# Seven products of block sums for 4 of 16 k tiles of gate/up, and the turn of hid on the tensor engine

## The chip, the cores and the metric

One of the eight cores of a Trainium2 chip runs the whole kernel. The metric is the device time of one launch in microseconds (us), as the median of three runs. The profile is of one execution. Its engines are PE (TensorE, matmuls; PEld is its weight load), DVE (VectorE), ACT (ScalarE), POOL (GpSimd) and SP, which only issues DMAs.

## The reference, cut to what matters

256 tokens of width 2048 pass a sparse attention layer, a layer norm, and a SwiGLU block of hidden width 5632. The change is in the SwiGLU:

```python
x = _layer_norm(DEEPNORM_ALPHA * x + m, ln1_g, ln1_b)             # 256 x 2048, m from the mixer
x = _layer_norm(DEEPNORM_ALPHA * x + (silu(x @ w_gate) * (x @ w_up)) @ w_down, ln2_g, ln2_b)
```

with w_gate and w_up 2048 x 5632 and w_down 5632 x 2048, all float32.

## The kernel before

**Precision.** Every weight is split in two parts of the tensor engine's rounded fp32 type: ACT copies raw to `w_hi` (L627), and DVE takes raw minus `w_hi` as `w_lo` (L903). A product of a 128x128 tile of activations (stationary) and 128x512 of weights (moving) is three matmuls: x_hi by w_hi, x_hi by w_lo, x_lo by w_hi (`product`, L1324 to L1331).

**Gate/up.** The hidden width is cut into 22 tiles of 256 columns (TILES). For a tile, 256 gate and 256 up columns stand side by side: a k tile's weights are 128x512. There are 16 k tiles (KD) and two groups of 128 tokens (TOK), so a tile is 16 x 2 x 3 = 96 matmuls into two PSUM banks of `acc`, with the pair of banks alternating from tile to tile. The weights come in loads of 1 MB (4 k tiles) into a ring `raw` of 4 slots; each load is split in two halves of 2 k tiles, and the split halves stand in rings of 4 (`w_hi`, `w_lo`). A half is thus 12 matmuls, and a tile 8 halves. SP issues a load when both halves of the load four places before it are split (`load`, L392). ACT may write a half's place when PE has used the half four before it (L626).

**After a tile.** While PE works on the next tile, ACT writes `sig` = silu(gate) (L686), DVE `hid` = `sig` times up (L1037), DVE turns `hid` into `turned` by 16 instructions that transpose 32x32 blocks (L1047), ACT writes the hi part of `turned` into `hid_t` (L690) and DVE the lo part (L1053). PE has no part in this. Tile 0 is worked out in an order of its own, between the halves of the layer norm (`first_tile`, L1470 to L1495); tile 1 follows (L1510), and then a loop over pairs of tiles (L1511). PE itself turns the layer norm's result into `act_t` by transposes against `ident` (L1420).

**Down.** Then 4 column groups of 512, each 44 k tiles of `hid_t` by 2 token groups by 3 matmuls (L1527 on). Each engine runs its instructions in the order in which they are written; a wait on a semaphore holds up all that stands behind it on that engine, SP's loads too.

Of the kernel before, what the change touches and what calls it, by code (L numbers as in the profile page):

```python
# [24 lines left out]
F32 = mybir.dt.float32  # L25
# [107 lines left out]
USED_DOWN = USED_FFN + 3 + (TILE_HALVES - 1) * (TILES - 1)  # L133
# [20 lines left out]
def layer_kernel(nc, a):  # L154
    ctx = ExitStack()
    with ctx:
# [7 lines left out]
        raw = sb("raw", [P, RING, RAW_ELEMS])  # L164
# [84 lines left out]

        ssq = small[:, 0:4]  # L250
# [17 lines left out]
        raw_full = [sem(f"raw_full{i}") for i in range(RING)]  # L268
# [68 lines left out]
        ffn_lo = sem("ffn_lo")  # L337
        y_scaled = sem("y_scaled")
# [5 lines left out]
            .rearrange("p (n e) -> p n e", e=IN_COLS)  # L344
        hid_flat = hid_t[:].rearrange("p k h s -> p (k h s)")
# [4 lines left out]
        w_out_rows, w_gu_rows, w_down_rows = flat("w_out"), flat("w_gu"), flat("w_down")  # L350

# [10 lines left out]
        def hid_of(i, x):  # L362
            tile = hid_flat[:, bass.ds(i * 4 * S, 4 * S)].rearrange("p (c x s) -> p c x s", c=2, x=2)
            return tile[:, :, x, :]

# [25 lines left out]
        def _(sp):  # L391
# [32 lines left out]
            with sp.Fori(0, TILES) as i:  # L424
                for j in range(RING):
                    load(R_FFN + RING * i + j, j, RAW_ELEMS,
                         w_gu_rows[bass.ds(i * P, P), j * RAW_ELEMS:(j + 1) * RAW_ELEMS])

            def load_down(g, b):
                k0, k1 = DOWN_K0[2 * b], DOWN_K0[2 * b] + DOWN_K[2 * b] + DOWN_K[2 * b + 1]  # L430
                load(R_DOWN + DOWN_BLOCKS * g + b, b % RING, (k1 - k0) * GC,
                     w_down_rows[bass.ds(g * P, P), k0 * GC:k1 * GC])
# [25 lines left out]
        def _(act):  # L458
# [162 lines left out]
            def hi_loop(used, raw_count, half, slot, n=HALF, first=None):  # L621
# [5 lines left out]
                act.activation(w_hi[:, (2 * slot + half) % RING, 0:n], raw[:, slot, first:first + n],  # L627
                               ACT.Copy).then_inc(hi_done, 1)
# [55 lines left out]
            def silu_step(i, c):  # L684
                act.wait_ge(ffn_full, i + 1)
                act.activation(sig[:], acc[:, 2 * c:2 * c + 2, 0:FC], ACT.Silu).then_inc(ffn_sig, 1)  # L686

            def hid_hi(i):
                act.wait_ge(ffn_turned, i + 1)
                act.activation(hid_of(i, 0), turned[:], ACT.Copy).then_inc(ffn_hi, 1)  # L690

            def ffn_tile(i, c):
                for h in range(TILE_HALVES):
                    used = used_ffn(i - 1, h + RING) if h < RING else used_ffn(i, h - RING)
                    hi_loop(used, fills(R_FFN + h // 2) + i, h % 2, h // 2)
                    if h == 3:
                        silu_step(i - 1, 1 - c)
                    if h == 6:
                        hid_hi(i - 1)

            ffn_tile(1, 1)
            with act.Fori(1, TILES // 2) as i:
                ffn_tile(2 * i, 0)
                ffn_tile(2 * i + 1, 1)


            def down_half(h, g):
                n = len(DOWN_K)
                used = used_down(g, h - 4) if h >= 4 else \
                    used_ffn(TILES - 1, h + 4) if isinstance(g, int) and g == 0 else used_down(g - 1, h + n - 4)  # L710
                hi_loop(used, fills(R_DOWN + h // 2) + DOWN_BLOCKS // RING * g, h % 2, h // 2 % RING,
                        n=DOWN_K[h] * GC, first=h % 2 * HALF)

            for h in range(len(DOWN_K)):
                down_half(h, 0)
                if h == 3:
                    silu_step(TILES - 1, 1)
                if h == 6:
                    hid_hi(TILES - 1)
# [6 lines left out]
            for h in range(HELD + RING, len(DOWN_K)):  # L726
                if h % 2 == 0:
                    act.wait_ge(raw_full[h // 2 % RING],
                                16 * fills(R_DOWN + DOWN_BLOCKS * (COL_GROUPS - 1) + h // 2))
# [14 lines left out]
        def _(dve):  # L744
# [154 lines left out]
            def lo_loop(v, half, slot, n=HALF, first=None):  # L899
                first = half * n if first is None else first  # L900
                dve.wait_ge(hi_done, v + 1)
                h = (2 * slot + half) % RING
# [132 lines left out]
            def gate_up(i, c):  # L1035
                dve.wait_ge(ffn_sig, i + 1)
                dve.tensor_tensor(hid[:], sig[:], acc[:, 2 * c:2 * c + 2, FC:2 * FC], ALU.mult).then_inc(ffn_hid, 1)  # L1037

            def turn_hid(i, to):

                if to[0] == 0:
                    dve.wait_ge(ffn_hid, i + 1)
                for b in to:
                    for n in range(4):
                        src = hid[32 * n:32 * n + 32, :, :].rearrange("p t (c f) -> p t c f", c=2)
                        dst = turned[32 * b:32 * b + 32, :, :].rearrange("p c (t s) -> p t c s", t=TOK)
                        last = dve.transpose(dst[:, :, :, 32 * n:32 * n + 32], src[:, :, :, 32 * b:32 * b + 32])  # L1047
                if to[-1] == 3:
                    last.then_inc(ffn_turned, 1)

            def hid_lo(i):
                dve.wait_ge(ffn_hi, i + 1)
                dve.tensor_tensor(hid_of(i, 1), turned[:], hid_of(i, 0), ALU.subtract).then_inc(ffn_lo, 1)  # L1053

            def ffn_tile(i, c):
                for h in range(TILE_HALVES):
                    lo_loop(2 * R_FFN + TILE_HALVES * i + h, h % 2, h // 2)
                    if h == 3:
                        gate_up(i - 1, 1 - c)
                        turn_hid(i - 1, (0, 1))  # L1060
                    if h == 4:
                        turn_hid(i - 1, (2, 3))
                    if h == 6:
                        hid_lo(i - 1)

            ffn_tile(1, 1)
            with dve.Fori(1, TILES // 2) as i:
                ffn_tile(2 * i, 0)
                ffn_tile(2 * i + 1, 1)


            for g in range(COL_GROUPS):
                for h in range(len(DOWN_K)):
                    v, n = 2 * R_DOWN + len(DOWN_K) * g + h, DOWN_K[h] * GC
# [3 lines left out]
                    else:  # L1078
                        lo_loop(v, h % 2, h // 2 % RING, n=n, first=h % 2 * HALF)
                    if g == 0 and h == 3:  # L1080
                        gate_up(TILES - 1, 1)
                        turn_hid(TILES - 1, (0, 1))
                    if g == 0 and h == 4:
                        turn_hid(TILES - 1, (2, 3))
                    if g == 0 and h == 6:
# [40 lines left out]
        def _(pool):  # L1126
# [39 lines left out]
            pool.wait_ge(xt_full, TOK * CHUNKS)  # L1166
# [5 lines left out]
        def _(pe):  # L1172
# [324 lines left out]
            def ffn_tile(i, c):  # L1497

                if not (isinstance(i, int) and i == 1):
                    pe.wait_ge(ffn_hid, i - 1)  # L1500
                for h in range(TILE_HALVES):
                    pe.wait_ge(lo_done, 2 * R_FFN + TILE_HALVES * i + h + 1)
                    for n in range(2):
                        for t in range(TOK):
                            last = product(2 * c, t, act_t, 2 * h + n, (w_hi, w_lo), h % RING, n,
                                           (h, n) == (0, 0), (h, n) == (TILE_HALVES - 1, 1))
                    last.then_inc(*((pe_used, 1) if h < TILE_HALVES - 1 else (ffn_full, 1)))

            first_tile()
            ffn_tile(1, 1)  # L1510
            with pe.Fori(1, TILES // 2) as i:  # L1511
                ffn_tile(2 * i, 0)
                ffn_tile(2 * i + 1, 1)


            def down_half(g, h, tokens):

                parts = (down_hi, down_lo) if g == COL_GROUPS - 1 and h >= HELD + RING else (w_hi, w_lo)
                for n in range(DOWN_K[h]):
                    k = DOWN_K0[h] + n  # L1520
                    for t in tokens:
                        paused = g == COL_GROUPS - 1 and t == 1 and h == HELD - 1 and n == DOWN_K[h] - 1
                        last = product(2 * (g % 2), t, hid_t, k, parts, h % RING, n, k == 0,
# [3 lines left out]
            def down_group(g):  # L1527
# [3 lines left out]
                pe.wait_ge(ffn_hid, TILES - 1 + g % 2)  # L1531
                held = HELD if g == COL_GROUPS - 1 else len(DOWN_K) - 1
                for h in range(held):
                    pe.wait_ge(lo_done, 2 * R_DOWN + len(DOWN_K) * g + h + 1)
                    if g == 0 and h == 0:
                        pe.wait_ge(ffn_lo, TILES - 1)
                    down_half(g, h, both).then_inc(pe_used, 1)
                for t in both:
                    if g == COL_GROUPS - 1 and t == 1:
                        pe.wait_ge(res_done, 2 * TOK * COL_GROUPS - 1)  # L1540
                    for h in range(held, len(DOWN_K)):
                        if t == 0:
                            pe.wait_ge(lo_done, 2 * R_DOWN + len(DOWN_K) * g + h + 1)
# [58 lines left out]
```

## Time and profile before

| what | us |
|---|---|
| median of 3 runs (lowest, highest) | 953.99 (953.26, 954.17) |
| span of the profiled execution, first to last instruction | 952.0 |
| PE busy in the profiled execution | 946.2 |
| DVE busy | 633.8 |
| ACT busy | 441.9 |
| tiles 1 to 21 and down, one unbroken stretch of PE | 696.33 |

The profiled execution has only its span; no time of the whole launch is recorded for it. The median of the runs is 2.0 us above the span. A matmul's duration in the profile is its latency: the next one starts before it ends, so what a matmul costs PE in a stream is read from start to start.

### The profile page before, as it was taken

To read this page: it belongs to the slowest core of one execution; us is meant where nothing else is said; L and a number is where in the kernel's file an instruction comes from. 1 tells how busy PE (TensorE), PEld (TensorE's weight loads), DVE (VectorE), ACT (ScalarE), POOL (GpSimd) and SP (SyncE) were. 2 spreads that over 40 slices of the span, in tenths; PEclk is the share of its full clock that TensorE was granted. 3 is DMA by queue.
4 is the path that set the end of the run, shared out by engine and by line. 5 is a ranking of instruction groups with operands and counts; after the bars stand their busy time and mean duration, and the time that the engine had idled before them with its cause. 6 is when DMAs were issued, how large, how long until landed. Compare 5 with 4: busy or idle time off the path is not lost.

```text
span 952.0 us, 12299 instructions
## 1 busy us (share of the span) xinstructions
PE 946.2 (99%) x4508; PEld 793.8 (83%) x4508; DVE 633.8 (67%) x1012; ACT 441.9 (46%) x573; POOL 40.9 (4%) x43
## 2 busy tenths in 40 slices
PE   9999999999999999999999999999999999999997
PEld 8999988888888888888888888888888888888885
DVE  6778566588776677777776776677775454554556
ACT  5676764362544444444444444444444343343450
POOL 0105530000000000000000000000000000000000
PEclk9999999999999999999999999999999999999999
DMA  9735225583365555554455555545457465464632
GB/s 365 318 140 177 97 82 185 209 347 142 108 219 204 180 203 190 186 209 178 176 184 211 204 193 185 210 178 194 181 209 291 141 232 188 160 237 156 225 129 88
DMA packets 28128, 183.57 MB, mean 193 GB/s; under 512 B 3136, under 2 KB 3648, under 8 KB 8640
## 3 DMA queue, kind: packets, MB, share of 16 engines
q1 hardware_dynamic: 28064, 183.12, 52.7%
q8 instruction: 22, 0.36, 0.2%
q14 instruction: 10, 0.08, 0.0%
q0 software_dynamic: 32, 0.00, 0.0%
HBM read 181.01 MB, written 2.10 MB: 192 GB/s over the span
## 4 chain that ended last, share of the span: by engine, by line
PE 99%; DVE 0%; ACT 0%; DVEq 0%; issue 0%; ACTq 0%
PE acc L1327 82%; PE acc L1265 5%; PE acc L1186 4%; PE acc L1464 2%; PE acc L1299 1%; PE tp L1378 1%; PE tp L1313 1%; PE tp L1391 1%; PE tp L1175 0%; PE tp L1404 0%; PE tp L1403 0%; PE tp L1402 0%; PE tp L1420 0%; PE acc L1555 0%; PE tp L1233 0%; DVE stats L1107 0%
## 5 line engine op out<-in xcount | busy, mean ns | idle before, releaser
L903 DVE TENSOR_TENSOR w_lo<-raw,w_hi 128x1024 fp32r<-128x1024 f32 (+1 forms) x283 | 335.3, 1194 | 242.4 <-ACT w_hi L627 240.6
L627 ACT ACTIVATE w_hi<-raw 128x1024 fp32r<-128x1024 f32 (+1 forms) x276 | 285.7, 1036 | 403.2 <-PE acc L1327 401.1
L1327 PE MATMUL acc<-w_hi,act_t 128*128 128x512 f32 x1344 | 413.9, 389 | 0.0
L1327 PEld LDWEIGHTS acc<-w_hi,act_t 128*128 128x128 f32 x1344 | 252.3, 188 | 52.5
L1327 PE MATMUL acc<-w_lo,act_t 128*128 128x512 f32 x672 | 261.4, 389 | 0.0
L1327 PE MATMUL acc<-w_hi,hid_t 128*128 128x512 f32 x672 | 207.2, 389 | 0.0
L1327 PEld LDWEIGHTS acc<-w_lo,act_t 128*128 128x128 f32 x672 | 126.1, 188 | 26.1
L1327 PEld LDWEIGHTS acc<-w_hi,hid_t 128*128 128x128 f32 x672 | 126.1, 188 | 26.1
L1327 PE MATMUL acc<-w_lo,hid_t 128*128 128x512 f32 x336 | 130.7, 389 | 0.0
L1047 DVE STREAM_TRANSPOSE turned<-hid 32x128 f32<-32x128 f32 x352 | 106.6, 303 | 5.6
L1327 PEld LDWEIGHTS acc<-w_lo,hid_t 128*128 128x128 f32 x336 | 63.1, 188 | 13.2
L1327 PE MATMUL acc<-w_hi,o_t 128*128 128x512 f32 x224 | 73.4, 398 | 0.0
L1327 PEld LDWEIGHTS acc<-w_hi,o_t 128*128 128x128 f32 x224 | 42.1, 188 | 8.6
L1327 PE MATMUL acc<-w_lo,o_t 128*128 128x512 f32 x112 | 43.6, 390 | 0.0
L779 DVE TENSOR_TENSOR w_lo<-raw,w_hi 128x1024 fp32r<-128x1024 f32 x24 | 29.1, 1219 | 7.7 <-ACT w_hi L489 7.7
L1265 PE MATMUL acc<-cq_t,w_hi 128*128 128x256 f32 x160 | 31.1, 289 | 0.0
L489 ACT ACTIVATE w_hi<-raw 128x1024 fp32r<-128x1024 f32 x24 | 25.0, 1051 | 3.9 <-DMA raw<-in_w_qidx 3.9
L1162 POOL TENSOR_SCALAR prob<-prob,row_inv 128x128 f32<-128x128 f32 (+1 forms) x24 | 25.2, 1063 | 26.7 <-DVE row_inv L877 26.7
L1265 PEld LDWEIGHTS acc<-cq_t,w_hi 128*128 128x128 f32 x160 | 25.2, 188 | 1.1 <-issue 1.0
L1327 PEld LDWEIGHTS acc<-w_lo,o_t 128*128 128x128 f32 x112 | 21.1, 188 | 4.1
L866 DVE TENSOR_TENSOR o_t<-tp,o_t 128x256 fp32r<-128x256 f32 x16 | 6.8, 425 | 25.1 <-ACT o_t L604 25.1
L1265 PE MATMUL acc<-cq_t,w_lo 128*128 128x256 f32 x80 | 22.5, 281 | 0.0
(179 smaller groups left out, 740.1 us busy)
## 6 DMA issues: line engine op xcount, KB each, us to landing
raw<-in_w_gu SPq DMA_DIRECT2D x88, 1024.0 KB, 4.8
raw<-in_w_down SPq DMA_DIRECT2D x32, 1024.0 KB, 4.6
raw<-in_w_out SPq DMA_DIRECT2D x16, 1024.0 KB, 4.8
raw<-in_w_down SPq DMA_DIRECT2D x16, 768.0 KB, 4.0
raw<-in_x_w SPq DMA_DIRECT2D x14, 552.0 KB, 7.1
raw<-in_w_uq SPq DMA_DIRECT2D x4, 1024.0 KB, 6.0
raw<-in_w_ukv SPq DMA_DIRECT2D x4, 1024.0 KB, 5.7
ln_rows<-in_ln_rows SPq DMA_DIRECT2D x4, 1024.0 KB, 7.3
```

Source lines behind the costliest of these rows:

```text
L489: act.activation(split_place(v)[0][:, v % RING, :], raw[:, r % RING, half * HALF:(half + 1) * HALF], ACT.Copy).then_inc(hi_done, 1)
L627: act.activation(w_hi[:, (2 * slot + half) % RING, 0:n], raw[:, slot, first:first + n], ACT.Copy).then_inc(hi_done, 1)
L779: dve.tensor_tensor(w_lo[:, v % RING, :], raw[:, r % RING, half * HALF:(half + 1) * HALF], w_hi[:, v % RING, :], ALU.subtract).then_inc(lo ...
L903: dve.tensor_tensor(w_lo[:, h, 0:n], raw[:, slot, first:first + n], w_hi[:, h, 0:n], ALU.subtract).then_inc(lo_done, 1)
L1047: last = dve.transpose(dst[:, :, :, 32 * n:32 * n + 32], src[:, :, :, 32 * b:32 * b + 32])
L1162: pool.tensor_scalar(prob[:, s % 3, cols], prob[:, s % 3, cols], row_inv[:, (s + 1) % 2, t:t + 1], None, ALU.mult).then_inc(prob_done, 1)
L1186: last = pe.matmul(acc[:, 2 * t + b, 0:c1 - c0], x[:, tok], w[:, c0:c1], start=(k == 0 and x is hi_ and w is hi_), stop=(k == KD - 1 and x ...
L1265: last = pe.matmul(out, part[:, v % RING, e0:e0 + P], act_tiles[:, k, x, :], start=(half == 0 and k == 0 and x == 0 and part is hi_), stop ...
L1299: last = pe.matmul(acc[:, (m + t) % 4, :], ckv_t[:, k, x, t * P:(t + 1) * P], wp[:, v % RING, k * 512:(k + 1) * 512], start=(n == 0), stop ...
L1313: last = pe.matmul(tp[:, h % 4, c0:c0 + n], qidx_t[rows, h // 2, t * P:(t + 1) * P], kidx_t[rows, 0:n], start=True, stop=True)
L1327: last = pe.matmul(acc[:, bank0 + t, :], lhs[:, k, x, t * P:(t + 1) * P], part[:, w, n * GC:(n + 1) * GC], start=(start and x == 0 and par ...
L1464: done = pe.matmul(acc[:, bank, :], act_t[:, k, x, t * P:(t + 1) * P], parts[part][:, w, n * GC:(n + 1) * GC], start=((h, n, x, part) == ( ...
```

## The change

**Seven products.** Tiles 2 to 21 are now done as 10 pairs (PAIRS - 1). For the first 4 of 16 k tiles (PAIR_K, two groups `q` of two k tiles, QUADS), the block product of 2 token groups x 2 k tiles by 2 k tiles x 2 tiles is worked out from seven products (`strassen`) in place of eight. Each product covers both groups `q`: 6 matmuls. The sums of activation blocks (`s_t`) are made once, by POOL and ACT. The sums of weight blocks are made in `raw` by DVE (`t_sum`), four a pair. Partial results pass from bank to bank by ACT's copies (`seed`, three a pair); the fifth result is copied to `p5_s` by ACT and added to two banks by DVE. The other 12 k tiles go as before (`plain`, 6 halves for each tile of the pair). The bank that the seeds leave from is written by products 0, 2 and 4, each only after the seed of the one before.

**The turn.** `hid` is turned by four PE transposes a tile into PSUM bank `tp[:, 3]` (`turn_hid`), for all 22 tiles; DVE's 16 instructions go. `sig` goes too: silu is written to `hid`.

**Loads.** `raw` has 5 slots: slots 0 to 2 carry the plain loads, slots 3 and 4 the two 1 MB loads of a pair's quads. In tiles 0 and 1 slots 0 to 3 are used as before. The bytes loaded are the same. The loop over pairs is written out on all engines.

PE:

```diff
+            def turn_hid(i):
+                pe.wait_ge(ffn_hid, i + 1)
+                if i > 0:
+                    pe.wait_ge(ffn_lo, i)
+                for c in range(2):
+                    for t in range(TOK):
+                        last = pe.transpose(turned[:, c, t * P:(t + 1) * P], hid[:, t, c * P:(c + 1) * P], ident[:])
+                last.then_inc(ffn_turned, 1)
+            def strassen(p, n, what, out, start):
+                v = v_pair(p, n)
+                pe.wait_ge(lo_done, v + 1)
+                for q in range(QUADS):
+                    for x, part in ((0, w_hi), (0, w_lo), (1, w_hi)):
+                        last = pe.matmul(out, factor(q, what, x), part[:, v % RING, q * GC:(q + 1) * GC],
...
+                last.then_inc(pe_used, 1)
+            def pair(p):
...
+                strassen(p, 0, "a11", u, True)
+                pe.wait_ge(s_lo, 1)
+                if p > 1:
+                    pe.wait_ge(p5_done, p - 1)
+                strassen(p, 1, "s1", p5, True)
+                pe.wait_ge(seeded, 3 * p - 2)
+                strassen(p, 2, "s2", u, False)
+                strassen(p, 3, "a12", first[:, 0, :], False)
+                pe.wait_ge(seeded, 3 * p - 1)
+                strassen(p, 4, "s3", u, False)
+                strassen(p, 5, "s4", second[:, 0, :], False)
+                pe.wait_ge(seeded, 3 * p)
+                strassen(p, 6, "a22", first[:, 1, :], False)
+                for h in range(PLAIN):
+                    if h == 0 and p > 1:
+                        turn_hid(2 * p - 2)
+                    if h == 5:
+                        turn_hid(2 * p - 1)
+                    plain(p, h, first)
+                pe.wait_ge(p5_added, 2 * p)
+                for h in range(PLAIN, 2 * PLAIN):
+                    plain(p, h, second)
```

In tile 1, `turn_hid(0)` stands ahead of half 5. ACT (`seed` copies a bank; `hi_product` is the split of one product's weights):

```diff
+            def tile_1():
...
+                    if h == 6:
+                        hid_hi(0)
+                        act.wait_ge(s_step, 5)
+                        act.activation(s_t[:, 0, :, :, :], s_sum[:], ACT.Copy).then_inc(s_hi, 1)
+            def hi_pair(p):
+                for q in range(QUADS):
+                    act.wait_ge(raw_full[PAIR_RING + q], 16 * quad_fill(p, q))
+                hi_product(p, 0, B11)
+                act.wait_ge(t_done, 4 * (p - 1) + 1)
+                hi_product(p, 1, B11)
+                act.wait_ge(t_done, 4 * (p - 1) + 3)
+                hi_product(p, 2, B11)
+                hi_product(p, 3, B21)
+                act.wait_ge(ffn_hid, 2 * p - 1)
+                seed(p, 0, first[:, 0, :], 1.0)
+                hi_product(p, 4, B12)
+                hi_product(p, 5, B22)
...
+                act.activation(p5_s[:], tp[:, 2, :], ACT.Copy).then_inc(p5_done, 1)
+                seed(p, 2, second[:, 0, :], -1.0)
+                act.wait_ge(t_done, 4 * p)
+                hi_product(p, 6, B21)
+                hi_plain(p, 0)
+                seed(p, 4, first[:, 1, :], 1.0)
+                for h in range(1, 2 * PLAIN):
+                    hi_plain(p, h)
```

DVE, POOL's sums and SP:

```diff
+            def lo_pair(p):
+                lo_product(p, 0, B11)
+                t_sum(B11, B11, B12)
+                t_sum(B12, B12, B22)
+                lo_product(p, 1, B11)
+                t_sum(B11, B11, B22)
+                lo_product(p, 2, B11)
+                lo_product(p, 3, B21)
+                t_sum(B21, B11, B21)
+                lo_product(p, 4, B12)
+                lo_product(p, 5, B22)
+                lo_product(p, 6, B21)
+                for h in range(2 * PLAIN):
+                    lo_plain(p, h)
...
+            pool.wait_ge(xt_lo, TOK * CHUNKS)
...
+            pool.tensor_tensor(x1_t[:], first_k[:, :, :, 0, :], first_k[:, :, :, 1, :], ALU.add).then_inc(s_step, 1)
...
+            pool.wait_ge(s_hi, 1)
+            pool.tensor_tensor(s_t[:, 1, :, :, :], s_sum[:], s_t[:, 0, :, :, :], ALU.subtract).then_inc(s_lo, 1)
...
+            def load_quads(p):
+                if p > 1:
+                    sp.wait_ge(lo_done, v_pair(p - 1, PRODUCTS))
+                for q in range(QUADS):
+                    if p == 1 and q == 0:
+                        sp.wait_ge(lo_done, V_FFN + 2 * TILE_HALVES)
+                    sp.dma_start(raw[:, PAIR_RING + q, :],
+                                 w_pairs[p - 1][:, q * RAW_ELEMS:(q + 1) * RAW_ELEMS])\
+                      .then_inc(raw_full[PAIR_RING + q], 16)
```

SP's order is `load_plain(1, 0..2)`, `load_quads(1)`, `load_quads(2)`, `load_plain(1, 3..5)`, and then for each later pair p three plain loads, `load_quads(p + 1)`, three plain loads.

## Rows read from the trace of the kernel before

**Rows 1.** The page: span, and busy time by engine.

```profile
span 952.0 us, 12299 instructions
PE 946.2 (99%) x4508; PEld 793.8 (83%) x4508; DVE 633.8 (67%) x1012; ACT 441.9 (46%) x573; POOL 40.9 (4%) x43
```

**Rows 2.** The chain that ended last: start, us, engine, tensor, line, count.

```profile
242.35 5.47 PE acc L1464 x24
247.83 696.33 PE acc L1327 x3072
```

**Rows 3.** Timeline of PE around one turn by transposes (start, us).

```profile
217.78 0.39 PE L1327 MATMUL acc<-w_hi,o_t 128*128 128x512 f32 x1
218.01 0.60 PE L1420 MATMUL tp<-ident,xn 128*128 128x128 f32 x4
218.37 0.48 PE L1327 MATMUL acc<-w_hi,o_t 128*128 128x512 f32 x1
...
219.61 0.39 PE L1327 MATMUL acc<-w_hi,o_t 128*128 128x512 f32 x1
```

**Rows 4.** Groups of PE by form: busy us, mean ns of one.

```profile
L1420 PE MATMUL tp<-ident,xn 128*128 128x128 f32 x32 | 4.8, 272 | 0.0
```

**Rows 5.** Timeline inside the loop over pairs of tiles, one half's period.

```profile
394.74 1.06 ACT L627 ACTIVATE w_hi<-raw 128x1024 fp32r<-128x1024 f32 x1 [1.66 <-PE acc L1327]
...
395.84 1.23 DVE L903 TENSOR_TENSOR w_lo<-raw,w_hi 128x1024 fp32r<-128x1024 f32 x1 [1.50 <-ACT w_hi L627]
...
397.24 0.33 SPq L394 DMA_DIRECT2D raw<-in_w_gu  x1
...
397.46 1.06 ACT L627 ACTIVATE w_hi<-raw 128x1024 fp32r<-128x1024 f32 x1 [1.66 <-PE acc L1327]
```

**Rows 6.** DMA issues on the page: KB each, median us from issue to landing.

```profile
raw<-in_w_gu SPq DMA_DIRECT2D x88, 1024.0 KB, 4.8
```

**Rows 7.** A window with several loads under way; last columns: PEclk, DMA share, GB/s.

```profile
708.00:710.00 2.00, 2.00 (x10) 1.66 (x9) 1.93 (x6) 1.30 (x2) 0.00 (x0) 1.00 1.02 422
```

**Rows 8.** Timeline of ACT and of DVE around the start of tile 1, several in a row.

```profile
242.39 0.60 ACT L665 ACTIVATE act_t<-tp 128x512 fp32r<-128x512 f32 x1 [2.61 <-PE tp L1420]
242.88 2.95 ACT L627 ACTIVATE w_hi<-raw 128x1024 fp32r<-128x1024 f32 x3
...
243.02 0.69 DVE L985 TENSOR_TENSOR act_t<-tp,act_t 128x512 fp32r<-128x512 f32 x1 [2.52 <-ACT act_t L665]
...
257.93 2.36 DVE L903 TENSOR_TENSOR w_lo<-raw,w_hi 128x1024 fp32r<-128x1024 f32 x2
```

**Rows 9.** Groups of ACT, DVE and POOL by form: busy us, mean ns of one.

```profile
L498 ACT ACTIVATE k_t<-acc 128x512 f32<-128x512 f32 x8 | 4.5, 588 | 1.7 <-PE acc L1265 1.7
L1047 DVE STREAM_TRANSPOSE turned<-hid 32x128 f32<-32x128 f32 x352 | 106.6, 303 | 5.6
L1153 POOL TENSOR_TENSOR more_lo<-raw,more_hi 128x1024 fp32r<-128x1024 f32 x4 | 9.6, 2398 | 41.5 <-DVE score L838 41.1
L1162 POOL TENSOR_SCALAR prob<-prob,row_inv 128x256 f32<-128x256 f32 x12 | 18.3, 1522 | 0.0
```

**Rows 10.** Timeline of PE in the first 9 us: warming matmuls, then the first of 512 columns.

```profile
0.77 3.75 PE L1175 MATMUL tp<-const-float32-0.0 128*128 128x256 f32 x8 [0.77 <-PEq L1591]
4.35 1.19 PE L1186 MATMUL acc<-in_hi 128*128 128x512 f32 x2
5.34 1.05 PE L1186 MATMUL acc<-in_hi,in_lo 128*128 128x512 f32 x2
6.19 0.69 PE L1186 MATMUL acc<-in_lo,in_hi 128*128 128x512 f32 x2
...
7.65 0.62 PE L1186 MATMUL acc<-in_hi 128*128 128x512 f32 x2
8.11 0.62 PE L1186 MATMUL acc<-in_hi,in_lo 128*128 128x512 f32 x2
```

More of the change, by code:

```diff
@@ L429, in load_down @@
+            for p in range(1, PAIRS):
+                if p == 1:
+                    load_plain(p, 0)
+                    load_plain(p, 1)
+                    load_plain(p, 2)
+                    load_quads(p)
+                else:
+                    for n in range(PAIR_RING):
+                        load_plain(p, n)
+                if p < PAIRS - 1:
+                    load_quads(p + 1)
+                for n in range(PAIR_RING, PLAIN_LOADS):
+                    load_plain(p, n)
             def load_down(g, b):
@@ L430, in load_down @@
                 k0, k1 = DOWN_K0[2 * b], DOWN_K0[2 * b] + DOWN_K[2 * b] + DOWN_K[2 * b + 1]
-                load(R_DOWN + DOWN_BLOCKS * g + b, b % RING, (k1 - k0) * GC,
-                     w_down_rows[bass.ds(g * P, P), k0 * GC:k1 * GC])
+                slot, n = b % RING, DOWN_BLOCKS * g + b
+                if isinstance(g, int) and n < RING:
+                    n_pair = PRODUCTS if slot == PAIR_RING else PRODUCTS + 2 * (slot + PAIR_RING) + 2
+                    sp.wait_ge(lo_done, v_pair(PAIRS - 1, n_pair))
+                else:
+                    sp.wait_ge(lo_done, V_DOWN + 2 * (n - RING) + 2)
@@ L434, in _ @@
+                sp.dma_start(raw[:, slot, 0:(k1 - k0) * GC],
+                             w_down_rows[bass.ds(g * P, P), k0 * GC:k1 * GC]).then_inc(raw_full[slot], 16)
             for b in range(RING):
@@ L619, in _, with hi_loop @@
                     hi_static(SPLIT_OF[s])
-            def hi_loop(used, raw_count, half, slot, n=HALF, first=None):
+            def hi_loop(used, raw_count, half, slot, n=HALF, first=None, shift=0):
                 first = half * n if first is None else first
@@ L626, in hi_loop @@
                 act.wait_ge(*used)
-                act.activation(w_hi[:, (2 * slot + half) % RING, 0:n], raw[:, slot, first:first + n],
+                act.activation(w_hi[:, (2 * slot + half + shift) % RING, 0:n], raw[:, slot, first:first + n],
                                ACT.Copy).then_inc(hi_done, 1)
@@ new lines, in hi_product, with hi_plain @@
+            def hi_product(p, n, block):
+                act.wait_ge(*before_pair(p, n))
+                act.activation(by_quad(w_hi[:, v_pair(p, n) % RING, :]), quad(block),
+                               ACT.Copy).then_inc(hi_done, 1)
+            def hi_plain(p, h):
+                n, slot = PRODUCTS + h, h // 2 % PAIR_RING
+                if h % 2 == 0:
+                    act.wait_ge(raw_full[slot], 16 * plain_fill(p, h // 2))
+                act.wait_ge(*before_pair(p, n))
+                act.activation(w_hi[:, v_pair(p, n) % RING, :], raw[:, slot, h % 2 * HALF:(h % 2 + 1) * HALF],
+                               ACT.Copy).then_inc(hi_done, 1)
@@ new lines, in seed @@
+            def seed(p, n, dst, sign):
+                act.wait_ge(*used_pair(p, n))
+                act.activation(dst, banks_of(2 * p + 1)[:, 1, :], ACT.Copy, scale=sign).then_inc(seeded, 1)
+            def hi_pair(p):
+                first, second = banks_of(2 * p), banks_of(2 * p + 1)
+                for q in range(QUADS):
[11 more added lines that the diff above has]
+                if p > 1:
+                    act.wait_ge(p5_added, 2 * (p - 1))
+                act.wait_ge(*used_pair(p, 1))
+                act.activation(p5_s[:], tp[:, 2, :], ACT.Copy).then_inc(p5_done, 1)
[6 more added lines that the diff above has]
+                    hi_plain(p, h)
+                    if h == 3:
+                        if p > 1:
+                            hid_hi(2 * p - 2)
+                        silu_step(2 * p - 1)
+                    if h == 9:
+                        hid_hi(2 * p - 1)
+                        silu_step(2 * p)
@@ L707, in down_half @@
+            tile_1()
+            for p in range(1, PAIRS):
+                hi_pair(p)
             def down_half(h, g):
@@ L1032, in _, with gate_up @@
             turned_lo(1, 3)
-            def gate_up(i, c):
+            def gate_up(i):
                 dve.wait_ge(ffn_sig, i + 1)
[L1037 to L1049, printed above, removed]
+                dve.tensor_tensor(hid[:], hid[:], banks_of(i)[:, :, FC:2 * FC], ALU.mult).then_inc(ffn_hid, 1)
@@ new lines, in plain @@
+            def plain(p, h, out):
+                n = PRODUCTS + h
+                v, k0 = v_pair(p, n), PAIR_K + 2 * (h % PLAIN)
+                pe.wait_ge(lo_done, v + 1)
+                for m in range(2):
+                    for t in range(TOK):
+                        for x, part in ((0, w_hi), (0, w_lo), (1, w_hi)):
+                            last = pe.matmul(out[:, t, :], act_t[:, k0 + m, x, t * P:(t + 1) * P],
+                                             part[:, v % RING, m * GC:(m + 1) * GC], start=False,
+                                             stop=((h % PLAIN, m, x) == (PLAIN - 1, 1, 1)), skip_group_check=True)
+                last.then_inc(*((ffn_full, 1) if h % PLAIN == PLAIN - 1 else (pe_used, 1)))
@@ L1509, in _ @@
             first_tile()
[L1510 to L1513, printed above, removed]
+            tile_1()
+            for p in range(1, PAIRS):
+                pair(p)
             def down_half(g, h, tokens):
-                parts = (down_hi, down_lo) if g == COL_GROUPS - 1 and h >= HELD + RING else (w_hi, w_lo)
+                late = g == COL_GROUPS - 1 and h >= HELD + RING
+                parts, w = ((down_hi, down_lo), h % RING) if late else ((w_hi, w_lo), (h + DOWN_POS) % RING)
@@ L1578 @@
     gate, up = (w[n].reshape(D, TILES, FC) for n in ("l0_ffn_gate", "l0_ffn_up"))
+    gu = k_tiles(np.stack([gate, up], axis=2).reshape(D, 2 * FFN), 2 * FC)
+    later = gu[2:].reshape(PAIRS - 1, 2, P, KD, 2 * FC)
+    quads = later[:, :, :, 0:PAIR_K].reshape(PAIRS - 1, 2, P, QUADS, 2, 2 * FC).transpose(0, 2, 3, 1, 4, 5)
+    plain = later[:, :, :, PAIR_K:].transpose(0, 2, 1, 3, 4).reshape(PAIRS - 1, P, -1)
     arrays = {
```

247 lines of the change are left out of this document (183 added, 64 removed).

## The prediction

> **What bounds the kernel now.** I read the page first: PE is busy for 946.2 of 952.0 us, with DVE at 633.8 and ACT at 441.9 [rows 1]. Then the chain that ended last: from the start of tile 1 to the end of the down product it is one stretch of PE, 3072 matmuls in 696.33 us, with no other engine in it [rows 2]. The reader is to see that nothing waits there, and what a matmul costs: 696.33 / 3072 = 0.2267 us. A half of 12 matmuls is then 2.72 us, which is also the spacing of ACT's splits, 394.74 to 397.46 [rows 5]. So only two things can move the time: matmul slots taken from or given to PE, and places where PE comes to wait. DVE's 106.6 us of 32x32 transposes [rows 9] are hidden under PE, so their removal is worth nothing by itself.
>
> **Removed from PE.** A pair was 2 x 96 = 192 matmuls. It is now 7 x 6 = 42 for the products and 2 x 12 x 2 x 3 = 144 for the rest, 186. Ten pairs save 60 matmuls: 60 x 0.2267 = 13.6 us. The new matmuls have the old shape (128x512), so I take the same price.
>
> **Added to PE.** Four transposes a tile, 22 tiles. One set of four like it stands in the trace between matmuls [rows 3]: from 217.78 to 219.61, 1.83 us, lie four transposes and six matmul slots (1.36 us), so the set costs 0.47 us. 22 x 0.47 = 10.3 us. Net on PE: -13.6 + 10.3 = -3.3 us. The operation is the same (128x128 fp32 against `ident`), so I leave this price without a range, except for the rival below.
>
> The Trainium skill ("TensorE: Matmul & The Clock Gate", Part 4) gives some 275 ns for one transpose in a kernel. The trace shows the same number as the duration, 272 ns [rows 4], but start to start the row above gives under half of it. By 272 ns each the 88 transposes would cost 23.9 us.
>
> **A steady pair (2 to 10).** Does PE wait in the short products? A product is 1.36 us of PE, but needs a split by ACT and one by DVE, and there are three seeds, one copy and four sums. I use spacings in a row: ACT 0.94 us for 1024 elements and 0.49 for 512, DVE 1.13 for 1024 (2.95 us for three, 242.39 to 242.88, 2.36 for two, each less the last one's full duration) [rows 8], and for the handing on the full durations 1.06 [rows 5], 0.59 [rows 9] and 1.23 [rows 5] with 0.04 us of signal (394.74 + 1.06 to 395.84). ACT starts 0.19 us after the next matmul could start. With product 0 at time 0, ACT may split it from -7.97, when PE has left the half four before. DVE: lo 0 at -6.87, two sums, lo 1 at -3.37, sum, lo 2 at 0.13, lo 3 at 1.29, sum, lo 4 at 3.55 (done 4.8, wanted 5.44), lo 5 done 5.9 (wanted 6.80), lo 6 done 7.3 (wanted 8.16). ACT: split 3 at 0.19, first seed 1.55 to 2.15 (wanted 2.72), splits 4 and 5, copy of product 1 at 3.94, second seed 4.43 to 5.03 (wanted 5.44), split 6, split of plain half 0 at 5.87, third seed 6.99 to 7.6 (wanted 8.16). Every step is in time, the tightest by 0.4 us. The lead over PE built up in the plain halves (2.72 us of PE for 1.13 of DVE) covers it. I take 0 us, with up to 0.5 us a pair as the other bound (a writing of PSUM by ACT is in no row; the nearest is ACT's reading of PSUM, 588 ns [rows 9]). The next pair's quads are issued a whole pair ahead, some 40 us for a landing of 4.8 us [rows 6]. Hidden too.
>
> **The first pair.** Here the lead is missing. The quads of pair 1 use slot 3 of `raw`, which in tile 1 holds halves 6 and 7, so SP issues them only when half 7 of tile 1 is split; SP's queue holds nothing else back, the plain loads of pair 1 stand ahead. Times from the start of tile 1 (247.83 [rows 2]):
> PE starts half 5 at 5 x 2.72 + 0.47 = 14.1 after the turn, half 7 at 19.5, and is done with the tile at 22.2. ACT has split half 6 at 9.4 and then stands at the hi part of tile 0's turned hid, which PE turns only ahead of half 5: it runs at 14.3. Behind it come the copy into `s_t` at 14.8 and the split of half 7 at 15.7, ready at 16.8. DVE's lo is ready at 18.0, in time for PE (19.5). SP issues 0.17 later (397.07 to 397.24 [rows 5]): 18.2. One load lands 4.8 us after its issue [rows 6]; with 422 GB/s [rows 7] the second needs 1.05 MB / 422 GB/s = 2.5 us more, so both are there at 25.5. ACT's split 1.1, DVE's lo 1.3: product 0 can start at 27.9. **PE waits 27.9 - 22.2 = 5.7 us.**
> POOL's sums are in time: they start at 243.71 [rows 8], four us ahead of the tile, and take 2.4 us for the 1024 elements and at most 1.5 each for the four of 256 [rows 9], done by 4.3 where ACT wants them at 14.8.
>
> From there the seven products go at the pace of the chain, with nothing prepared. From product 0: sum ready at 1.1, split 1 ready 2.2, lo 1 at 3.5; third sum 4.6, split 2 5.7, lo 2 7.0, first seed (behind split 3) 7.2; products start at 0, 3.5, 7.2, 8.6, then 10.4 (lo 4 behind lo 3 and the fourth sum), 11.8, 13.1 and end at 14.5, where steady they end at 9.5. **5.0 us more.** In the plain halves ACT and DVE are ahead again. Bounds for the two together: 8.7 (a landing of both in 5.3 us, no waits beyond the sums) and 12.7 (a landing of both in 9.3 us).
>
> **The clock.** The granted clock is 1.00 in the window of [rows 7], as everywhere in the stretch at issue. But the matmuls of the first 6 us after idleness took about twice as long: 8.11 - 7.65 = 0.46 for two, against about 1 us for two at 4.35 and 5.34 [rows 10]; that is the lower of the two levels (1.2 and 2.4 GHz) and then the upper. That spell lasted from 0.77 to some 6.2 us, 5.4 us of nearly steady work. After a wait of 5.7 us and products with gaps of 2 us, it can come again. Products 0 and 1 at half speed would be hidden in their own waits; if the 5.4 us count only from product 2 on, 12 matmuls take 5.4 in place of 2.7 us: +2.7. If products 0 and 1 count (2 x 2.72 = 5.4), or the clock doesn't fall: 0. I take the middle, 1.4 us.
> The same page of the Trainium skill (Part 1) says that idleness brings the array back to 1.2 GHz and that only sustained work lifts it; no stretch between the start and the end of this trace has such a gap. By that rule the clock falls here, and the sum ends nearer to its upper than to its lower bound.
>
> **Other edits, at nothing.** silu into `hid` instead of `sig` has to wait for the turn before it, which PE does a few us after DVE wrote hid, and hid's next writing is a tile later. In the down product two turns stand at halves 1 and 7, their parts wanted at half 22. The code written out rather than looped: down is written out before and its 1056 matmuls show no wait [rows 2].
>
> **Sum.** 952.0 - 13.6 + 10.3 + 5.7 + 5.0 + 1.4 = 960.8 us of span; the median of runs stands 2.0 above the profiled span, so 962.8 us, 0.9% slower.
>
> **Rivals.**
> 1. *The first pair's loads are in time* (faster). The wait at slot 3 is the deciding place: if the quads were split and their sums made before 22.2, only -3.3 is left: 950.7. For it: the raw ring has a fifth slot, and one quad needs no old slot. Against it: that quad stands behind the other on SP, and the split of product 0 waits for both. It would decide if the wait and the chain together cost under 1.4 us; they are at 10.7.
> 2. *Every pair waits at a seed or a sum.* If ACT's or DVE's steps cost 0.15 us more than taken, each of the later seeds passes its margin of 0.4 to 0.5 us: up to 0.5 us in nine pairs, +4.5: 967.3. For it: the margins are thin; against: DVE's relief of 106.6 us.
> 3. *The clock stays low through the first pair*, all products from 2 on at 2.72 us: 7.2 + 5 x 2.72 = 20.8 in place of 14.5, 6.3 us, 4.9 above my term: 967.7.
> 4. *The transposes hold PE for their full duration*: + 23.9 - 10.3 = +13.6: 976.4. This is the page's price; the start-to-start row speaks against it.
>
> **Chances and range.** Forecast 0.70, rival 1 0.05, rival 2 0.10, rival 3 0.08, rival 4 0.03; 0.04 for a first pair partly hidden, near no change. The forecast's own bounds are 960.8 - 1.4 - 2.0 + 2.0 = 959.4 and 960.8 + 1.3 + 2.0 + 2.0 = 966.1; with rivals 2 and 3 the range is 958 to 969, which leaves out some 0.15. This kernel's measurement tells 0.2%, 1.9 us. Faster 0.05, same 0.04, slower 0.91.
>
> **What the profile after would show.** 60 fewer 128x512 matmuls and 88 transposes at 0.11 us from start to start. One gap of PE of about 5.7 us some 22 us after the start of tile 1, ended by DVE's lo of product 0, behind ACT, behind a DMA of the quads issued near 266. Gaps of 2 us before products 1 and 2. No gap in pairs 2 to 10. A granted clock below 1.00 only just behind the gap. Wrong would be: quads issued before half 7's lo; waits on `seeded` in every pair; transposes spaced by 0.27.

## The result, and the profile after

The changed kernel took 963.52 us (962.64 to 964.98, 4 runs) against 954.02 us before: a ratio of 1.0104, 95% interval 1.009 to 1.0119. It is 1.0% slower; forecast were 962.8 us. The profiled execution has a span of 962.8 us, 10.8 above that of before [rows 1].

The page after, to set beside [rows 1]:

```profile
span 962.8 us, 11466 instructions
PE 949.2 (99%) x4536; PEld 794.4 (83%) x4536; DVE 624.6 (65%) x750; ACT 486.4 (51%) x644; POOL 52.2 (5%) x49
PE   9999999999969999999999999999999999999997
```

PE has 28 more instructions (60 matmuls fewer, 88 transposes more) and one slice of forty with a hole. Every new wait is in that slice; the transposes are spread over all tiles. The chain that ended last (start, us, what), where the one unbroken stretch of [rows 2] stood:

```profile
264.31 2.59 DVE w_lo L1090
266.90 0.02 issue
266.91 4.68 DMA raw<-in_w_pairs
271.60 2.50 issue
274.09 1.06 ACT w_hi L836
275.16 0.02 issue
275.18 1.23 DVE w_lo L1242
276.41 2.27 DVE raw L1254 x2
278.68 1.21 DVE w_lo L1242
...
283.60 9.79 PE acc L1769 x30
293.39 13.60 PE acc L1782 x60
306.99 0.44 PE tp L1738 x4
307.43 19.07 PE acc L1782 x84
326.50 4.08 PE tp L1769 x18
...
412.75 4.08 PE tp L1769 x18
```

Read it downwards: DVE's lo of tile 1's last half (L1090) lets SP issue the two quads of pair 1; the first lands after 4.68 us and the second some 2.5 us later (the row marked `issue`, in which ACT waits for both); ACT and DVE split product 0; DVE makes the sums. Only from 283.6 on is the chain PE again, and then it stays PE to the down product's end. From pair 2's start (326.50) to pair 4's (412.75) are 86.25 us, 43.1 a pair, with not one wait; before, two tiles were 192 x 0.2267 = 43.5.

PE in pair 1 (timeline; the last bracket is the idle time before the row and who ended it):

```profile
269.59 0.39 PE L1750 MATMUL tp<-w_hi,act_t 128*128 128x512 f32 x1
276.56 0.76 PE L1769 MATMUL acc<-w_hi,act_t 128*128 128x512 f32 x1 [6.58 <-DVE w_lo L1242]
...
280.04 0.77 PE L1769 MATMUL tp<-w_hi,s_t 128*128 128x512 f32 x1 [0.59 <-DVE w_lo L1242]
...
283.60 0.80 PE L1769 MATMUL acc<-w_hi,s_t 128*128 128x512 f32 x1 [0.66 <-ACT acc L851]
...
293.23 0.39 PE L1782 MATMUL acc<-w_hi,act_t 128*128 128x512 f32 x1
```

PE could have started product 0 at 269.59 + 0.23 = 269.82 and started at 276.56: a wait of 6.7 us. The seven products then took 293.23 - 276.56 = 16.7 us, where a later pair takes 9.5: 7.1 us more. Windows of pair 1; of the last three columns the first is the granted clock:

```profile
270.00:276.00 6.00, 0.00 (x0) 0.00 (x0) 0.82 (x1) 1.06 (x1) 0.00 (x0) 0.69 0.53 224
276.00:278.00 2.00, 1.44 (x4) 1.19 (x5) 2.00 (x3) 0.42 (x1) 0.00 (x0) 0.50 0.00 0
...
288.00:290.00 2.00, 2.00 (x7) 1.58 (x6) 1.22 (x1) 0.93 (x2) 0.00 (x0) 0.67 0.00 0
290.00:292.00 2.00, 2.00 (x10) 1.63 (x9) 1.22 (x1) 1.56 (x3) 0.00 (x0) 1.00 0.85 279
```

The clock fell to half (1.2 GHz) during the wait and came back near 289.3, after 5.7 us of PE work without a gap. The sum: -3.3 (PE's work) + 6.7 + 7.1 = +10.5, against 10.8 measured.

One row was not forecast. DVE's and POOL's timelines around the late lo:

```profile
257.06 1.23 DVE L1090 TENSOR_TENSOR w_lo<-raw,w_hi 128x1024 fp32r<-128x1024 f32 x1 [1.55 <-ACT w_hi L755]
262.42 0.69 DVE L1228 TENSOR_TENSOR hid_t<-tp,hid_t 128x512 fp32r<-128x512 f32 x1 [4.13 <-ACT hid_t L820]
264.31 2.58 DVE L1090 TENSOR_TENSOR w_lo<-raw,w_hi 128x1024 fp32r<-128x1024 f32 x1 [1.20 <-ACT w_hi L755]
```

```profile
263.41 2.40 POOL L1398 TENSOR_TENSOR s_t<-s_sum,s_t 128x1024 fp32r<-128x1024 f32 x1 [10.61 <-ACT s_t L831]
```

The same subtraction took 1.23 us at 257.06 and 2.58 us at 264.31, where POOL's of the same size was running when it started. POOL's ended at 265.81 and DVE's at 266.89, 1.08 us later.

### The profile page after: what moved, and what is told of

Its sections match the earlier page's. It is cut to its first block, busy times and chain, and to the rows that moved or that the text cites. A ratio compares the mean times of both kernels' runs of the same rounds, so it can differ in the third digit from the quotient of the medians.

```text
span 962.8 us, 11466 instructions
## 1 busy us (share of the span) xinstructions
PE 949.2 (99%) x4536; PEld 794.4 (83%) x4536; DVE 624.6 (65%) x750; ACT 486.4 (51%) x644; POOL 52.2 (5%) x49
## 4 chain that ended last, share of the span: by engine, by line
PE 70%; DVE 1%; DMA 0%; ACT 0%; issue 0%; DVEq 0%; ACTq 0%
PE acc L1782 26%; PE acc L1561 25%; PE tp L1782 8%; PE acc L1769 6%; PE tp L1769 4%; PE tp L1738 1%; DMA raw<-in_w_pairs 0%; DVE raw L1254 0%; PE acc L1867 0%; DVE w_lo L1090 0%; DVE w_lo L1242 0%; ACT w_hi L836 0%; ACT w_hi L755 0%; DVE stats L1326 0%; ACT acc L851 0%
## 5 line engine op out<-in xcount | busy, mean ns | idle before, releaser
L1090 DVE TENSOR_TENSOR w_lo<-raw,w_hi 128x1024 fp32r<-128x1024 f32 (+1 forms) x123 | 146.1, 1195 | 133.8 <-ACT w_hi L755 133.1
L1782 PE MATMUL acc<-w_hi,act_t 128*128 128x512 f32 x720 | 227.1, 392 | 0.0
L1249 DVE TENSOR_TENSOR w_lo<-raw,w_hi 128x1024 fp32r<-128x1024 f32 x120 | 145.2, 1224 | 95.8 <-ACT w_hi L845 94.7
L755 ACT ACTIVATE w_hi<-raw 128x1024 fp32r<-128x1024 f32 x116 | 115.9, 1001 | 164.7 <-PE acc L1561 152.3
L845 ACT ACTIVATE w_hi<-raw 128x1024 fp32r<-128x1024 f32 x120 | 126.1, 1060 | 126.3 <-PE acc L1782 111.2
L1782 PEld LDWEIGHTS acc<-w_hi,act_t 128*128 128x128 f32 x720 | 135.2, 188 | 27.8
L1782 PE MATMUL acc<-w_lo,act_t 128*128 128x512 f32 x360 | 140.2, 389 | 0.0
L836 ACT ACTIVATE w_hi<-raw 128x1024 fp32r<-128x1024 f32 x70 | 72.9, 1057 | 74.4 <-DVE raw L1254 48.5
L1242 DVE TENSOR_TENSOR w_lo<-raw,w_hi 128x1024 fp32r<-128x1024 f32 x70 | 83.9, 1222 | 35.1 <-ACT w_hi L836 34.0
L1782 PEld LDWEIGHTS acc<-w_lo,act_t 128*128 128x128 f32 x360 | 67.7, 188 | 13.6
L1782 PE MATMUL tp<-w_hi,act_t 128*128 128x512 f32 x240 | 74.7, 389 | 0.0
L1254 DVE TENSOR_TENSOR raw<-raw 128x1024 f32<-128x1024 f32 x40 | 47.9, 1219 | 0.0
L1782 PE MATMUL tp<-w_lo,act_t 128*128 128x512 f32 x120 | 46.7, 389 | 0.0
L1769 PE MATMUL acc<-w_hi,act_t 128*128 128x512 f32 x100 | 36.9, 410 | 6.6 <-DVE w_lo L1242 6.6
```

Of the source, the lines that this page charges most:

```text
L755: act.activation(w_hi[:, (2 * slot + half + shift) % RING, 0:n], raw[:, slot, first:first + n], ACT.Copy).then_inc(hi_done, 1)
L836: act.activation(by_quad(w_hi[:, v_pair(p, n) % RING, :]), quad(block), ACT.Copy).then_inc(hi_done, 1)
L845: act.activation(w_hi[:, v_pair(p, n) % RING, :], raw[:, slot, h % 2 * HALF:(h % 2 + 1) * HALF], ACT.Copy).then_inc(hi_done, 1)
L1090: dve.tensor_tensor(w_lo[:, h, 0:n], raw[:, slot, first:first + n], w_hi[:, h, 0:n], ALU.subtract).then_inc(lo_done, 1)
L1242: dve.tensor_tensor(by_quad(w_lo[:, v % RING, :]), quad(block), by_quad(w_hi[:, v % RING, :]), ALU.subtract).then_inc(lo_done, 1)
L1249: dve.tensor_tensor(w_lo[:, v % RING, :], raw[:, h // 2 % PAIR_RING, h % 2 * HALF:(h % 2 + 1) * HALF], w_hi[:, v % RING, :], ALU.subtract) ...
```

## The experiments

The runs below are compared with runs of the kernel before on the same chip (median 953.62 us for the first four, 953.80 for the others).

**1. The hi part of hid later.** My theory: the wait is the late load, and the load is late because ACT stands at the turned hid before it splits half 7.

```diff
-                    if h == 6:
+                    if h == 7:
                         hid_hi(0)
                         act.wait_ge(s_step, 5)
```

(and `hid_lo(0)` on DVE behind half 7 too.)

> The changed kernel with the hi and lo parts of tile 0's turned hid, and the copy into s_t behind them, moved from behind half 6 to behind half 7 of tile 1. My theory (the wait ahead of pair 1 is the late load of its quads, held up by ACT standing at hid before it splits half 7): half 7 is split about 4.5 us earlier on ACT (at 258.7 instead of 263.2) and lo 7 is not slowed, so the quads are issued near 260.2 instead of 266.9, and the wait of 6.7 us ahead of product 0 shrinks to under 1 us; the granted clock stays 1.00, which gives 2 to 3 us more; the chain of sums and splits (5 us) stays. About 963.5 - 6.5 - 2.2 = 955 us. Rival (the wait is the chain from PE's last halves, whatever the loads do): no change, 963.5. Rival (the lower clock comes from the gaps between the products, not from the long wait): 957.

Measured: 958.2 us, ratio 1.0045 (1.0029 to 1.006). PE's timeline:

```profile
270.67 0.47 PE L1769 MATMUL acc<-w_hi,act_t 128*128 128x512 f32 x1 [0.71 <-DVE w_lo L1242]
...
274.16 0.47 PE L1769 MATMUL tp<-w_hi,s_t 128*128 128x512 f32 x1 [1.85 <-DVE w_lo L1242]
...
277.72 0.79 PE L1769 MATMUL acc<-w_hi,s_t 128*128 128x512 f32 x1 [1.94 <-ACT acc L851]
```

The quads were issued at 260.97 (lo 7 stood at 259.72 here, clear of POOL, and took 1.23 us) and the long wait went as forecast, to 0.7 us. So the wait is the load, not the chain of PE's last halves. But the time came down by only 5 us, not 8.5. In the profiled execution the clock fell all the same, near 275.7, as product 1 ended, and products 2 and 3 ran at half speed. A window of it:

```profile
276.00:282.00 6.00, 4.28 (x10) 3.41 (x11) 5.73 (x5) 5.38 (x8) 0.00 (x0) 0.50 0.00 0
```

Before the fall PE had been idle for 0.7 and for 1.85 us, no longer. My expectation had tied the clock to the long wait; that was wrong, and the rival on record (the clock falls by the gaps between the products, 957 us) was nearer. The clock is only a part of the miss of 3 us: the one run of four with a mean clock of 1.000 still took 957.43. Most of the rest, as these figures have it, is that the expectation took 2.2 us off for a clock that, by run 4, costs the changed kernel 0.6 in the median.

**2. The quads of pair 1 early, in a place of their own.**

```diff
+        raw_1 = at(base_r + 2 * 4 * S * 4)("raw_1", [P, QUADS, RAW_ELEMS])
...
                 if p == 1:
+                    load_quads(p)
                     load_plain(p, 0)
                     load_plain(p, 1)
                     load_plain(p, 2)
-                    load_quads(p)
```

(Their loads go into `raw_1` once the out product has left its place.)

> The changed kernel with pair 1's quads loaded into a place of their own (in hid_t's part that is written only from tile 2 on), issued before pair 1's plain loads, with a semaphore of their own. Theory: no wait ahead of product 0, products 1 and 2 wait little since their splits and sums begin ahead of them, clock 1.00. Of the 9.5 us lost only the net of PE's work stays, -3.3 us, with 0 to 2 us of waits left in pair 1: 951 to 953 us, faster than the kernel before by 0.1 to 0.35%. Rival (waits at seeds and sums are in every pair and hidden in the trace's reading): 956 or more.

Measured: 955.47 us (11 runs), ratio 1.0017 (1.0008 to 1.0026): the loss all but gone, the gain not there, so that both the 951 to 953 us forecast and the rival's 956 or more were missed. Product 0 started without a wait (269.26), but the products still took 12.9 us to 282.18, with a gap of 1.94 us ahead of product 2: DVE's lo 7 was as late as before (263.73, 2.59 us beside POOL), and the sums stand behind it. The 11 runs are of two kinds: three at 953.9 to 954.1 us with a mean granted clock of 1.000, eight at 955.2 to 956.0 with 0.998. The profiled execution is one of the three. So the second kind costs 1.6 us more; that this is a dip of the clock in pair 1 is read from the means and not shown by a trace.

**3. The turn on PE alone**, in the kernel before.

```diff
+                    if h == 3:
+                        if not (isinstance(i, int) and i == 1):
+                            pe.wait_ge(ffn_lo, i - 1)
+                        pe_turn(i - 1)
```

> The kernel before with one part of the change alone: hid turned by four PE transposes a tile into PSUM bank tp 3, ahead of half 3 of the next tile; no seven products. Theory (a set of four costs PE 0.47 us of its stream): 22 x 0.47 = 10.3 us slower, 964.3 us. Rival (full durations of 272 ns hold PE): 23.9 us slower, 978. Rival (DVE's relief gives something back): under 960.

Measured: 964.36 us, ratio 1.0111 (1.0096 to 1.0127), 10.7 us over before. Part of its chain:

```profile
256.51 21.81 PE acc L1321 x96
...
278.76 21.80 PE acc L1321 x96
...
301.00 21.81 PE acc L1321 x96
```

A tile is 278.76 - 256.51 = 22.25 us, 0.49 more than 96 x 0.2267 = 21.76. DVE's lighter load gives nothing back, and the transposes' full duration is not what PE pays.

**4. The waits of pair 1 filled** with matmuls into banks that are overwritten afterwards.

```diff
+                if p == 1:
+                    for n in range(28):
+                        pe.matmul(tp[:, 2, :], act_t[:, n % 4, 0, 0:P], act_t[:, 4:6, 0, :],
+                                  start=True, stop=True)
                 strassen(p, 0, "a11", u, True)
```

(and 8 more ahead of each of products 1 and 2.)

> The changed kernel with matmuls that go nowhere in pair 1's waits: 28 of 512 columns ahead of product 0, 8 ahead of product 1 and 8 ahead of product 2, into banks that are overwritten afterwards. The output is the same. They should end before the waits do (28 x 0.227 = 6.4 of 6.7 us; 1.8 of about 2.2). Theory (the clock fell because PE stood idle, and costs 2.2 us): granted clock 1.00 throughout, pair 1's products in 14.5 us instead of 16.7, 961.3 us, with up to 0.5 us either way for the last filler. Rival (the fall costs nothing because the products wait for ACT and DVE anyway): 963.5.

Measured: 962.89 us, ratio 1.0097. The granted clock was 1.00 in every window of pair 1, and PE's rows show

```profile
269.65 6.51 PE L1794 MATMUL tp<-act_t 128*128 128x512 f32 x28
276.47 0.50 PE L1769 MATMUL acc<-w_hi,act_t 128*128 128x512 f32 x1 [0.30 <-DVE w_lo L1242]
```

From product 0 to the first plain matmul (291.15) are 14.7 us, against 16.7 with the low clock. So of the 7.1 us that pair 1's products lose, the chain of splits and sums makes 5.2 and the clock 2.0. In the medians that is only 0.6 us, nearer to the rival (963.5, the fall costs nothing) than to the 961.3 expected, since the profiled execution of the changed kernel had the deepest dip of its four runs (mean clock 0.991 and 962.8 us of span; the others 0.993 to 0.996 and 961.8 to 960.5).

**5. Everything out of the way.** As 2, and in tile 1 the copy into `s_t` (and so POOL's subtraction) behind half 4, tile 0's turn ahead of half 4, its hi and lo parts behind half 7.

```diff
-                    if h == 6:
-                        hid_hi(0)
+                    if h == 4:
                         act.wait_ge(s_step, 5)
                         act.activation(s_t[:, 0, :, :, :], s_sum[:], ACT.Copy).then_inc(s_hi, 1)
+                    if h == 7:
+                        hid_hi(0)
```

> The early quads of pair 1, and in tile 1 the copy into s_t behind half 4 instead of half 6, the turn of tile 0's hid ahead of half 4 instead of 5, and its hi and lo parts behind half 7. Theory: what is left of the loss in pair 1 (products in 13.1 us where a later pair takes 9.5) is that lo 7 and with it lo 0 and the first two sums come 3 us late, half of it because ACT stands at the turned hid and half because DVE's subtraction runs at the same time as POOL's (2.6 instead of 1.2 us). With both out of the way pair 1 runs like the others, clock 1.00 in every run: 3.5 us under the fastest early-quads run, 950.3 us, a ratio to the kernel before of 0.9965. Rival (the first pair needs more lead than tile 1 can give): 952 or more, and gaps ahead of products 1 and 2.

Measured: 950.43 us, ratio 0.9967 (0.9955 to 0.9979), granted clock 1.000 in all six runs. The chain in pair 1 is PE alone:

```profile
258.44 10.93 PE tp L1761 x48
269.37 1.36 PE acc L1780 x6
270.73 1.36 PE tp L1780 x6
272.09 6.80 PE acc L1780 x30
278.89 13.60 PE acc L1793 x60
```

278.89 - 269.37 = 9.5 us, the steady value. The 3.4 us under the kernel before agree with the 3.3 us of PE's net work. (In the profiled executions tile 1 began at 247.12 here and at 247.83 before [rows 2], so agreement to a few tenths is as much as these two show.) The run moves several things together, and doesn't say what each is worth.

**6. The turn back on DVE in the changed kernel**, in two parts behind plain halves 1 and 2, and 6 and 7.

```diff
+                    if p > 1 and h in (1, 2):
+                        dve_turn(2 * p - 2, (2 * (h - 1), 2 * (h - 1) + 1))
...
+                    if h in (6, 7):
+                        dve_turn(2 * p - 1, (2 * (h - 6), 2 * (h - 6) + 1))
```

> The changed kernel with the turn of hid back on DVE, in halves behind plain halves 1 and 2 and 6 and 7 of a pair: the seven products alone. Theory: PE gets 10.3 us back, and since DVE turns tile 0's hid by 258, ACT no longer stands at it and the quads of pair 1 are issued near 261 instead of 267, which gives 5 us more: 963.5 - 10.3 - 5.3 = 948 us, plus 0 to 4 us where DVE's 2.5 us of transposes come too close to the short products. Rival (DVE has no room for both, so PE waits in every pair): over 955.

Measured: 952.08 us (10 runs), ratio 0.9985 (0.9975 to 0.9994), at the upper edge of what was expected. PE's 10 us came back; the 5 us of an earlier load didn't. DVE's timeline at tile 1:

```profile
243.55 8.36 DVE L1090 TENSOR_TENSOR w_lo<-raw,w_hi 128x1024 fp32r<-128x1024 f32 x4 [0.26 <-ACT w_hi L755]
...
261.16 2.88 DVE L1239 TENSOR_TENSOR hid_t<-turned,hid_t 128x512 fp32r<-128x512 f32 x1
263.96 1.21 DVE L1090 TENSOR_TENSOR w_lo<-raw,w_hi 128x1024 fp32r<-128x1024 f32 x1
```

Four subtractions took 8.36 us beside POOL's sums, as they did in the changed kernel from 243.85 (four in a row would be 3 x 1.13 + 1.23 = 4.6), and the one into `hid_t` 2.88 us beside POOL's 2.95 us from 260.55. ACT had split half 7 by 261.4, but its lo came at 263.96, the quads were issued at 265.20, and PE waited 5.9 us.

**7. Only ACT's copy into `s_t` moved**, and with it POOL's subtraction, away from lo 7.

```diff
+                    if h == 4:
+                        act.wait_ge(s_step, 5)
+                        act.activation(s_t[:, 0, :, :, :], s_sum[:], ACT.Copy).then_inc(s_hi, 1)
                     if h == 6:
                         hid_hi(0)
-                        act.wait_ge(s_step, 5)
-                        act.activation(s_t[:, 0, :, :, :], s_sum[:], ACT.Copy).then_inc(s_hi, 1)
```

> The changed kernel with one thing moved: ACT's copy into s_t, on which POOL's subtraction waits, stands behind half 4 of tile 1 instead of half 6. Theory: POOL's 2.4 us then lie beside another, early, lo of DVE; lo 7 takes 1.2 instead of 2.6 us and is split 0.95 us earlier, so the quads are issued 2.3 us earlier: wait ahead of product 0 of 4.4 instead of 6.7 us, 961 us. Rival (DVE's 2.6 us has another cause than POOL): lo 7 stays at 2.6 us, 962.5.

Measured: 962.03 us, ratio 1.0087. PE's wait is 4.6 us, and lo 7 is back at its length:

```profile
262.81 1.23 DVE L1091 TENSOR_TENSOR w_lo<-raw,w_hi 128x1024 fp32r<-128x1024 f32 x1 [0.26 <-ACT w_hi L755]
```

POOL's subtraction lay beside a pair of earlier lo's instead (254.34), and these took 3.72 us in place of 2.36 [rows 8]. The wait shrank by 2.0 of the 2.3 us forecast, of which 1.35 are lo 7's length and 0.95 the copy that no longer stands ahead of the split of half 7. The time missed the 961 us expected by one; the row of lo 7, not the time, decides against the rival. Here too the runs differ with the clock: 960.3 us at 0.998, 962.0 to 962.1 at 0.993.

**8. The seven products without PE's turn, with everything out of the way.**

> The seven products with pair 1's quads early, the s_t copy behind half 4, and hid turned by DVE. Theory: the full price of the 60 matmuls is kept: 953.8 - 13.6 = 940.2 us if DVE's work fits, up to 944 with 0.3 to 0.4 us of PE waiting a pair behind the transposes; ratio 0.986 to 0.990. Rival (DVE has no room): 950 or more.

The edits are those of 2 and 6, and the `s_t` copy behind half 4. Measured: 941.54 us (941.09 to 941.72), ratio 0.9871 (0.9856 to 0.9886), 12.3 us under the kernel before, of the 13.6 that 60 matmuls are worth. The list of waits has one in the products, 0.3 us, in pair 1:

```profile
PE acc L1800 <- DVE w_lo L1267: 0.3, 1, 0.3
```

From product 0 to the first plain matmul are 10.4 us (269.68 to 280.05), 0.9 above the steady 9.5; that is most of the 1.3 us missing from the 13.6. From pair 2 to pair 4 are 84.3 us (312.85 to 397.17), 42.2 a pair, which is 186 x 0.2267. DVE is now busy for 724.7 of 939.5 us, but it had room for both.

## Why the prediction was right, point by point

- *60 matmuls by 0.2267 us.* Right: 43.1 us a pair with the turns, 42.2 without (run 8). Run 8's time shows 12.3 of the 13.6 us.
- *0.47 us a set of four transposes.* Right: 0.49 by run 3's tiles, 10.7 us in all. The rival of 272 ns each (23.9 us) is dead; the transposes show a mean duration of 271 ns after as well, and don't hold PE for it.
- *A steady pair waits nowhere.* Right in all nine. The rival of a wait in every pair gave no row.
- *The wait ahead of pair 1, 5.7 us.* The mechanism was right: run 1 shifts the load and the wait follows. The size is 6.7. The term that was mis-sized is DVE's lo 7, taken at 1.23 us; it took 2.58 beside POOL's subtraction, and run 7 brings that row back to 1.23. I had costed POOL's work as to whether it came in time, and not as to what it does to DVE.
- *The chain without a lead, 5.0 us.* 5.2 at the full clock (run 4).
- *The clock, 1.4 us.* 2.0 in the profiled execution and 0.6 in the medians (run 4), of different depth from run to run. The sentence that the fall comes after the long wait and then gaps was too narrow: in run 1 idle times of 0.7 and 1.85 us were all that came before it. The 5.4 us of work at half speed, taken over from [rows 10], didn't hold either: the last section has how differently the clock came back. The Trainium skill ("TensorE: Matmul & The Clock Gate", Part 1) says that idleness brings the clock to 1.2 GHz and that activity releases it; this gave the right sign, and the trace agrees: 0.50 in the wait, 1.00 again from 289.3.
- *The hidden first load* (faster) was rightly given little: run 5 shows what it would have been, 950.4 us, where 950.7 was worked out.
- *Luck.* That 962.8 lies within 0.7 us of 963.52 is in part luck: the wait was 1.0 us, the turn 0.4 and the chain 0.2 too small, and the clock 0.8 too large for the median.

Why the changed kernel is slower is thus shown, not argued: the turn on PE takes back 10.3 of 13.6 us (10.7 by run 3), and pair 1 loses 13.8 us once (6.7 + 7.1). Most of that hangs on quads that wait for a slot which the tile before still holds (run 2). The last 3.4 us (12.9 against 9.5 in run 2's products) went only with run 5, which also moved ACT's and POOL's work away from half 7.

## What to carry to other kernels

A new stage that needs short work units lives on the lead that the long ones before it build up: look at its first instance, and ask when its first loads can be issued and what stands ahead on each queue. Before work is moved from an engine with room to the one that bounds the kernel, price it there start to start; here it ate three quarters of the gain, and run 8 shows that the engine it was taken from could keep it. A copy that feeds POOL can be moved by some microseconds for nothing; where it lies beside a critical two-input instruction of DVE it costs that instruction's length again.

## What was not expected of the hardware

POOL and DVE hold each other up, and by nearly whole instructions: DVE's 128x1024 subtraction took 2.58 in place of 1.23 us and ended 1.08 us after POOL's, which was running when it started. In run 6 it went both ways: POOL's subtraction, started at 260.55 beside a pair of DVE's that ran from 258.88 to 261.24, took 2.95 in place of 2.40 us; DVE's 128x512 one into `hid_t`, started at 261.16, ended 0.54 us after it and took 2.88 us, where the kernel before shows 0.68 at 260.21. POOL's 128x256 sums, which the prediction bounded at 1.5 us each, took 1.6 to 1.7 beside DVE's four subtractions, which took 8.36. An estimate: four sums at a quarter of POOL's 2.40 us, its first 2.41 us and DVE's four at 1.13 make 9.3 us one after another, and from the first's start to the last's end (243.68 to 252.81) are 9.1.

The Trainium skill ("GPSIMD Engine Reference", 1. Specifications) says that POOL's way to SBUF is shared with DVE and that DVE's instructions with two SBUF inputs contend for it; this trace agrees. DVE's multiplication into `hid`, which has one input in PSUM, met POOL's last sum in the changed kernel and was not held up (0.67 us; 0.69 in the kernel before at 250.87, with POOL idle):

```profile
251.21 1.60 POOL L1396 TENSOR_TENSOR s_sum<-x_t,s_sum 128x256 f32<-128x256 f32 x1
```

```profile
252.13 0.67 DVE L1224 TENSOR_TENSOR hid<-hid,acc 128x512 f32<-128x512 f32 x1
```

The granted clock can fall with PE idle for no more than 1.9 us at a time (run 1), and not in every run of one and the same program: run 1's mean is 0.996 in three runs and 1.000 in one. It comes back as unevenly: near 289.3 in the changed kernel, 12.7 us after product 0 started, and near 277.0 in run 7, 3.0 us after.
